# Modulation vectors of the first layer by 24 products of 512 columns, behind the mixer's first norm

## The reference

```
silu_c  = jax.nn.silu(c)            # (1, 1024)
silu_cc = jax.nn.silu(c_ctx)        # (1024,)
for i in range(DEPTH_2):            # 2 layers
    mod_l = silu_c  @ ada_w[i] + ada_b[i]     # ada_w[i]: (1024, 6144)
    mod_c = silu_cc @ ada_w[i] + ada_b[i]
    sh1, sc1, gt1, sh2, sc2, gt2 = split(mod_l, 6)
    hl = rmsnorm(x, norm1_g[i]) * (1 + sc1) + sh1
    ...
```

```
u = rms_norm(h, g_mix)
proj = u @ w_in
c_q, c_kv, k_pe, fox_qkv, f_logit = split(proj)
q  = rms_norm(c_q, g_cq) @ w_uq  ...    kv = rms_norm(c_kv, g_ckv) @ w_ukv ...
fq = rms_norm(fq, g_q_fox) ...          fk = rms_norm(fk, g_k_fox) ...
```

## Time and profile before

| | |
|---|---|
| median of 3 runs | 3297.79 us |
| the runs | 3297.67, 3304.46, 3297.79 us |
| the profiled execution: time | 3298.74 us |
| the profiled execution: span, first to last instruction | 3297.0 us |
| PE busy | 2788.6 us (85%) |
| PE weight loads busy | 1930.1 us (59%) |
| DVE, ACT, POOL busy | 1089.4, 507.5, 312.9 us |
| DMA | 616.54 MB, mean 187 GB/s |
| mean granted TensorE clock | 0.914 of full |

### The profile page before, as it was taken

One profiled execution on the slowest core, in us unless ns is written; L12 is line 12 of the kernel. 1 busy time (PEld: TensorE's weight loads), 2 busy tenths in 40 slices (PEclk: granted clock), 3 DMA queues, 4 the chain that ended last, 5 costly groups with the idle time before them and its releaser, 6 DMA issues. The chain is left out here.

```text
span 3297.0 us, 58116 instructions
## 1 busy us (share of the span) xinstructions
PE 2788.6 (85%) x25421; PEld 1930.1 (59%) x25421; DVE 1089.4 (33%) x2190; ACT 507.5 (15%) x1105; POOL 312.9 (9%) x342
## 2 busy tenths in 40 slices
PE   6998979899998997796877589889898976978775
PEld 5887835688685444543444234388887964534443
DVE  3563263256514322210100331265555522101102
ACT  1000112100010101100000100144444411000001
POOL 0000000000000000211111110032232201111110
PEclk9999765799999998798999789799999987989998
DMA  6685100377623203899999611000000018999994
GB/s 221 229 249 165 58 26 1 102 245 239 191 77 115 77 26 121 337 396 402 405 403 403 232 61 51 18 3 4 4 4 3 4 53 331 403 407 408 406 405 193
DMA packets 279699, 616.54 MB, mean 187 GB/s; under 512 B 28900, under 2 KB 182007, under 8 KB 245412
## 3 DMA queue, kind: packets, MB, share of 16 engines
q1 hardware_dynamic: 237584, 539.56, 44.1%
q10 hardware_dynamic: 30756, 59.18, 5.0%
q0 software_dynamic: 11120, 14.23, 1.3%
HBM read 612.76 MB, written 21.08 MB: 192 GB/s over the span
## 5 line engine op out<-in xcount | busy, mean ns | idle before, releaser
L2008 PE MATMUL bank<-expert_weights,ex_xt 128*64 128x256 f32 x2688 | 312.6, 388 | 96.3 <-DMA expert_weights<-in_moe_w_up_dram 72.4
L2008 PEld LDWEIGHTS bank<-expert_weights,ex_xt 128*64 128x64 f32 x2688 | 213.8, 140 | 209.7 <-issue 140.9
L455 PE MATMUL bank<-u,weights 128*128 128x272 f32 (+1 forms) x1408 | 318.3, 390 | 14.0 <-DVEq L478 14.0
L455 PEld LDWEIGHTS bank<-u,weights 128*128 128x128 f32 x1408 | 270.5, 192 | 61.8 <-DVEq L478 14.8
L1161 DVE SCALAR_TENSOR_TENSOR ada_acc<-ada_w,cond,ada_acc 128x512 f32 (+1 forms) x336 | 227.6, 745 | 1.6 <-PEq L427 1.6
L1919 DVE TENSOR_TENSOR ex_hidden<-ex_silu,bank 128x256 f32<-128x256 f32 x64 | 27.0, 421 | 596.4 <-ACT ex_silu L2057 572.1
L533 PE MATMUL bank<-rw_mixed,weights 128*128 128x512 f32 (+2 forms) x448 | 188.6, 582 | 31.7 <-DVEq L544 28.2
L2008 PE MATMUL bank<-weights,ex_xt 128*64 128x256 f32 x1408 | 165.9, 392 | 32.4 <-DMA weights<-in_moe_w_up_dram 31.0
L2029 PE MATMUL bank<-expert_weights,ex_hidden_turned 128*64 128x512 f32 x672 | 159.9, 619 | 21.7 <-DVE ex_hidden_turned L1922 21.7
L2008 PEld LDWEIGHTS bank<-weights,ex_xt 128*64 128x64 f32 x1408 | 111.5, 141 | 92.9 <-issue 54.2
L533 PEld LDWEIGHTS bank<-rw_mixed,weights 128*128 128x128 f32 (+1 forms) x448 | 83.9, 189 | 136.8 <-issue 134.9
(11 more groups left out here) (520 smaller groups left out, 4127.0 us busy)
## 6 DMA issues: line engine op xcount, KB each, us to landing
expert_weights<-in_moe_w_gate_dram SPq DMA_DIRECT2D x84, 1024.0 KB
expert_weights<-in_moe_w_up_dram SPq DMA_DIRECT2D x84, 1024.0 KB
expert_weights<-in_moe_w_down_dram SPq DMA_DIRECT2D x84, 1024.0 KB
ada_w<-in_ada_w_dram ACTq DMA_DIRECT2D x24, 2048.0 KB, 8.8
weights<-in_moe_w_gate_dram SPq DMA_DIRECT2D x44, 1024.0 KB
weights<-in_moe_w_up_dram SPq DMA_DIRECT2D x44, 1024.0 KB
weights<-in_moe_w_down_dram SPq DMA_DIRECT2D x44, 1024.0 KB
weights<-in_w_gate_dram SPq DMA_DIRECT2D x22, 1024.0 KB, 5.3
```

What stands on the lines that cost most here:

```text
L455: last = nc.tensor.matmul(k.bank[b + side * NB][:, 0:N], w[:, f, c * P:(c + 1) * P], rhs[:, f, 0:N], start=(f == 5), stop=(f == 4))
L2008: last = nc.tensor.matmul(half_cols(k.bank[2 + side], t), xt[:, s, f * SLOTS:(f + 1) * SLOTS], w[:, q * 512 + t * 256:q * 512 + t * 256 + ...
```

## The change

The first layer's vectors are made as the second layer's are. The 24 products stand behind the sums of the norm `mix`, the copy by ACT in the same block, the four transposes at the head of the input projection on PE, and bias and gains at its head on DVE. The 96 one-column products and the old `spread` are gone from `fqn`, `fkn`, `cq` and `ckv`. `mark` runs once, in the norm `mix`; `gm_norm` keeps its row sums but no longer writes or waits for `ada_one_of`. `ada_acc` is freed ahead of the input projection. Some parameters that nothing uses are dropped (`early`, `finish`, `mods` of the row norm).

```diff
@@ norm_stage @@
-            if mods is not None and mods.l == 1:
+            if mods is not None:
                 mods.keep_rows(act)
...
-            if mods is not None and mods.l == 0:
-                mods.sums(mods.share_of_norm)
-            if mods is not None and mods.l == 1:
+            if mods is not None:
                 mods.row_sums(pe)
...
-            if mods is not None and mods.l == 1:
+            if mods is not None and mods.l == 0:
                 mods.mark(dve)
...
-            if mods is not None and mods.l == 0 and mods.columns == 6 * DC:
-                mods.spread(dve)
@@ in_proj_stage @@
         def _(pe):
+            mods.turn_rows(pe)
             n = 0
...
         def _(dve):
+            mods.spread_rows(dve)
             for n, w in enumerate(widths):
@@ head_norm_stage @@
-            if mods is not None:
-                mods.sums(14)
@@ ModSums.row_sums @@
-        pe.wait_ge(self.marked, 2)
+        if self.l == 0:
+            pe.wait_ge(self.marked, 2)
@@ first_model @@
-            norm_stage(k, "mix", k.h, DC, D, EPS, [(0, TA, param(k, "g_mix", DC), None)], u)
-            in_proj_stage(k, seg["in"], u, proj)
+            norm_stage(k, "mix", k.h, DC, D, EPS, [(0, TA, param(k, "g_mix", DC), None)], u, mods=mods)
+            early.close()
+            in_proj_stage(k, seg["in"], u, proj, mods)
         head_norm_stage(k, "fqn", proj[:, 4:8, :], fqk[:, 0:4, :], P, 4, RH, k.head_ones, param(k, "g_q_fox"),
-                        RH ** -0.5, META, SEQ, mods)
+                        RH ** -0.5, META, SEQ)
...
-                   mods=mods)
-        early.close()
```

More of the change, by code:

```diff
@@ L487, in _, with linear_stage @@
             rounds(dve, seg.tiles, body)
-def linear_stage(k, name, seg, tile_chunks, rhs, N, write, banks, on_scalar=False, side=None, first=None, early=0, pool=None):
+def linear_stage(k, name, seg, tile_chunks, rhs, N, write, banks, on_scalar=False, side=None, first=None, pool=None):
     nc = k.nc
@@ L517, in _ @@
         def _(pe):
-            if early:
-                side.sums(early)
             def body(i, js):
@@ L593, in flat, with in_proj_stage @@
     return ap.rearrange("p a t -> p (a t)")
-def in_proj_stage(k, seg, u, proj):
+def in_proj_stage(k, seg, u, proj, mods):
     starts = [0, P, 2 * P, 3 * P] + [3 * P + ROPE + P * i for i in range(12)] + [3 * P + ROPE + 12 * P]
@@ L643, in _, with head_norm_stage @@
                 nc.vector.tensor_copy(proj[0:w, n, :], k.bank[n % 4][0:w, 0:TA]).then_inc(emptied, 1)
-def head_norm_stage(k, name, src, dst, rows, heads, width, ones, gain, factor, t0, N, mods=None):
+def head_norm_stage(k, name, src, dst, rows, heads, width, ones, gain, factor, t0, N):
     nc = k.nc
@@ L700, in _, with row_norm_stage @@
                                                op0=ALU.mult, op1=ALU.mult)
-def row_norm_stage(k, name, sides, per, width, mods=None):
+def row_norm_stage(k, name, sides, per, width):
     nc = k.nc
@@ L1127, in __init__ @@
         self.summed, self.done = k.sem("mod_summed"), k.sem("mod_done")
-        self.columns = self.parts = 0
-        self.share_of_norm = 10
         self.landed = [k.sem(f"ada_landed{s}") for s in range(2)]
         self.added = k.sem("ada_added")
-        if l == 1:
-            self.one_of, self.rows = k.ada_one_of, k.ada_rows
-            self.marked, self.kept = (k.sem(f"ada_{n}") for n in ("marked", "kept"))
+        self.one_of, self.rows = k.ada_one_of, k.ada_rows
+        self.marked, self.kept, self.turned = (k.sem(f"ada_{n}") for n in ("marked", "kept", "turned"))
     def load(self, eng, r, s):
@@ L1170, in last_share @@
         self.add(dve, self.begun - 1, self.ROUND - self.ROUND // self.rest, self.ROUND)
[L1172 to L1181, removed]
     def mark(self, dve):
@@ L1222, in spread_rows @@
         self.gains()
[L1224 to L1233, removed]
     def gains(self):
@@ L1242, in gains, with ffn @@
                                                in1=param(k, name, DC, DC * l), op0=ALU.add, op1=ALU.mult)
[L1244 to L1253, removed]
+def ffn(k, n, h, u, T, t0, seg, gains, to, acc):
     nc = k.nc
@@ L1265, in ffn @@
                          in1=flat(h[:, ds(m, 1), t0:T]), op0=ALU.mult, op1=ALU.add), 3,
-                     side=side, early=early)
+                     side=side)
     return side
@@ L1305, in first_model @@
         with nc.sbuf_tensor("u_mix", [P, DC, TA], F32) as u:
-            norm_stage(k, "mix", k.h, DC, D, EPS, [(0, TA, param(k, "g_mix", DC), None)], u)
-            in_proj_stage(k, seg["in"], u, proj)
+            norm_stage(k, "mix", k.h, DC, D, EPS, [(0, TA, param(k, "g_mix", DC), None)], u, mods=mods)
+            early.close()
+            in_proj_stage(k, seg["in"], u, proj, mods)
         head_norm_stage(k, "fqn", proj[:, 4:8, :], fqk[:, 0:4, :], P, 4, RH, k.head_ones, param(k, "g_q_fox"),
-                        RH ** -0.5, META, SEQ, mods)
+                        RH ** -0.5, META, SEQ)
         head_norm_stage(k, "fkn", proj[:, 8:12, :], fqk[:, 4:8, :], P, 4, RH, k.head_ones, param(k, "g_k_fox"),
-                        1.0, 0, TA, mods)
-        norm_stage(k, "cq", proj[:, 0:2, :], 2, 2 * P, EPS, [(0, TA, param(k, "g_cq", 2), None)], proj[:, 0:2, :],
-                   mods=mods)
-        norm_stage(k, "ckv", proj[:, 2:3, :], 1, P, EPS, [(0, TA, param(k, "g_ckv", 1), None)], proj[:, 2:3, :],
-                   mods=mods)
-        early.close()
+                        1.0, 0, TA)
+        norm_stage(k, "cq", proj[:, 0:2, :], 2, 2 * P, EPS, [(0, TA, param(k, "g_cq", 2), None)], proj[:, 0:2, :])
+        norm_stage(k, "ckv", proj[:, 2:3, :], 1, P, EPS, [(0, TA, param(k, "g_ckv", 1), None)], proj[:, 2:3, :])
         q = sb("q", [P, HEADS, TA])
```

## The result

| | before | after |
|---|---|---|
| median, 20 runs each, alternating | 3301.58 us | 3306.76 us |
| lowest to highest | 3295.94 to 3307.86 | 3300.64 to 3310.60 |
| ratio | | 1.0015, 95% interval 1.0009 to 1.0021 |
| the profiled execution: time, span | 3298.74, 3297.0 us | 3307.03, 3305.3 us |

The change makes the kernel slower by 5.0 us (3.0 to 6.9), 0.15%, reckoned from the ratio; the medians differ by 5.2 us. A second set of runs, 11 of the kernel after and 21 of the kernel before, gave 1.0009 (1.0000 to 1.0018), 3.0 us (0 to 5.9); its medians differ by 2.3 us. Both are less than the 0.2% that was called no change.

What follows compares the result with a forecast made beforehand. The stretch was taken as a chain of blocks, each bound by its slowest engine, with no transfer setting an end. Added 15.4, less 2.5 clock and 10.3 removal, gave +2.6 on a 3297.79 median: 3300.4 us, range 3296 to 3307.

Steps and rivals of the forecast that it cites:

- Row sums: Norm mix: 24 products from about 293.4, 20.8 us at full clock, only some 6 us beside the norm's DVE work.
- The projection 15.4 us later: Input projection: first real matmul at 315.5 instead of 300.1, behind row sums, copy and transposes; cost 15.4 us.
- The clock gives 2.5 us back: Head of the projection: no half clock for its first 5 us, as PE idles less in mix; gain 2.5, bounds 0 and 2.7.
- The removal gives 0, 0.05, 4.47 and 5.81 us: Blocks fqn, fkn, cq, ckv: time each could end sooner without its column products; 10.3 us in sum.
- The removal was to cost no clock: Later norms and expansion: clock was already at half with the column products, so removing them costs 0.
- The sum of 2.6: Whole kernel: 15.4 - 2.5 - 10.3 = +2.6 us, slower.
- The rest of the kernel moves as a whole: Behind the changed stretch: everything starts from a block's end, so it all shifts together by the +2.6 us.
- rival 1: Input projection: the clock does not come back, the pause at 314 being enough to lose it; +5.1 us, 3302.9; chance 0.09.
- high run: Whole kernel: median falling on a run like the 3304.46 one, one of three and 6.7 us above the others.
- rival 2: Expansion and after: clock comes up late with PE idle from ckv's last sum; +10.6 to +18.6 us; chance 0.08, 0.06 decide.
- (3): Attention: clock, 0.50 over 154 us, comes up in part as stages shift; saves up to 10 us, 3290.4; chance 0.06.
- (4): cq and ckv: something else holds them and nothing is freed; +12.9 us, 3310.7; chance 0.03.

## Why the prediction was right, point by point

- Row sums from 293.4, 20.8 us at full clock: 293.51 and 20.78. The copy 0.59: 0.59, ending at 314.92 against 314.8. Transposes 0.42: from the first transpose to the first product 0.32. The projection 15.4 us later: 315.54 - 300.13 = 15.41, of which 0.11 is start-up.
- The clock gives 2.5 us back: the first eviction is 13.0 us later, so 2.4. The row on which this leaned, the pause behind the second layer's row sums at full clock, was a poor witness: in the kernel after, the same pause is followed by half clock. Here the step held, with a pause of 0.93 us in mix. No experiment has lengthened this pause; that its being shorter than 2.1 us saved the step isn't shown.
- The removal gives 0, 0.05, 4.47 and 5.81 us: the kernel after is late by 12.93 us at cq's start, 8.46 at ckv's, 2.67 at the expansion's. The differences are 4.47 and 5.79. The bias and gains end at 316.53, 3 us ahead of the first eviction, so they are hidden.
- The removal was to cost no clock. It was at half in cq and ckv in both, as forecast, but stayed so for 4.1 us of the expansion against 3.1 before. The prediction put this at 0 with up to 2 us in its range; it is 0.4 us.
- The sum of 2.6 is thus right for the stretch: 2.67 at the expansion's first product, of which 0.11 is start-up, and 3.0 without it once the clock is up. "The rest of the kernel moves as a whole" was wrong. The order of the work does; but each later pause of PE at which the clock may fall is met in another position, and the steps add up to +3.2 before the experts. The ratios give 5.0 us (3.0 to 6.9) and 3.0 us (0 to 5.9). The first interval leaves the 2.6 out, the second has it inside. That the steps make up the difference to 2.6 is likely by the traces, but behind the experts no trace can show it.
- The forecast's absolute 3300.4 us started from a median of three runs, 3297.79. The median of 20 is 3301.58, 3.8 us higher. Of the 6.4 us to the measured 3306.76, this is the larger part, and it is no error of the mechanism. The range held the value, if only by 0.2 us, and that was luck: it reached to 3307 for rival 1 and for a high run, and neither came. The forecast's own range, 3298.3 to 3302.8 with a chance of 0.68, missed it, and as a difference the 5.2 us between the medians stand just above its +5.
- Rivals: the clock did come back for the projection (1). In the expansion it rose 1.0 us late and not 4 or more (2). Attention stayed at half (3). cq and ckv were freed (4). A clock that changes at another place, which rival 2 looked for in the expansion, cost more further on.

## What to carry to other kernels

Price a product by the columns that it streams or, if it streams a single one, by its weight load; 24 products of 512 columns are not cheap beside 96 of one. Put such side work where an engine idles beside another's chain, in pieces that fit each gap; here that turned +5 us into -13. And before a few microseconds are judged from two traces, pair the instructions of both: a step in a stage that was not touched, beside a change of the granted clock, may belong to the shift and not to the edit. A pure delay of the same size tells which.

## What the runs showed of the hardware

- A one-column float32 product costs about what its weight load of 128 columns does. 28 of them took 8.0 us with the clock at full for a part and 11.95 at half throughout. The tile's rows of the kernel before (shortest, median and longest record in ns):

```profile
L1177 PEld LDWEIGHTS bank<-ones,ada_acc x192: 190/333/338, 368.8 to 412.8; 128*128 128x128 f32 x192
L1177 PE MATMUL bank<-ones,ada_acc x192: 167/352/353, 369.0 to 412.9; 128*128 128x1 f32 x192
```

- A high busy share of PE in the profile doesn't mean a full clock. With PE busy in 12.68 of 13 us, nearly all by one-column products, the granted clock was 0.50; with PE busy in 3.00 of 3 us by the same products it was 1.00.
- A pause of PE of 2.1 us was followed by full clock or by half, by the place where the kernel met it: full in the kernel before and in the one that came to it 10.5 us later, half in those that came 2.5 to 6.1 us later.
- A pure delay of 1.7, 2.6 or 4.3 us at one place became 7.2 - 3.3 = 3.9, 9.9 - 3.3 = 6.6 and 13.1 - 3.2 = 9.9 us some 800 us later. Time lost is not handed on one to one. The values are read in gm_out, less what fkn had by then.
